# Relaying the hybrid-head stage of a two-block transformer kernel on half chunks

## The reference, cut to what matters

```python
def hybrid_layer(x, ...):
    h = rms_norm_2(x, g_norm)
    z = h @ w_in                         # 2656 columns
    aq, ak, av, ag, bq, bk, bv, bg, cq, ckv, ckr, cg = split(z)
    qa, ka = axial_rope(rms_norm_2(aq, a_qn)), axial_rope(rms_norm_2(ak, a_kn))
    oa = dense_gqa(qa, ka, av) * silu(ag)            # 6 heads, 2 kv heads, 64 wide
    qb, kb = rope(bq), rope(bk)
    ob = windowed_sink_gqa(qb, kb, bv, sink) * silu(bg)
    qc = rms_norm_2(cq, c_qn) @ c_wuq                # 4 heads, 64 + 32 wide
    kv = rms_norm_2(ckv, c_kvn) @ c_wukv
    oc = mla(qc, kv, rope(ckr)) * silu(cg)
    return x + concatenate([oa, ob, oc]) @ w_out     # 1024 by 1024
```

## Time and profile before

| what | value |
|---|---|
| median of three runs | 1870.01 us |
| lowest, highest | 1867.84, 1870.3 us |
| the profiled execution: its time, its span | 1870.01 us, 1868.2 us |
| TensorE busy | 1731.6 us, 93% of the span |
| VectorE busy | 1125.2 us, 60% |
| ScalarE busy | 794.7 us, 43% |
| mean granted TensorE clock | 0.961 of full speed |

### The profile page before, as it was taken

How to read it: one execution, slowest core, us unless ns; L and a number is a source line. 1 busy time by engine, 2 the same in 40 slices (tenths; PEclk the granted TensorE clock), 3 DMA queues, 4 the chain that set the end, 5 groups by cost and what they waited for, 6 DMA issues and landing times.

```text
span 1868.2 us, 28467 instructions
## 1 busy us (share of the span) xinstructions
PE 1731.6 (93%) x12340; PEld 1614.7 (86%) x12340; DVE 1125.2 (60%) x1317; ACT 794.7 (43%) x1011; POOL 41.1 (2%) x64
## 2 busy tenths in 40 slices
PE   7999988888999999999998888899999998889886
PEld 6999888878999999899988778899999997669765
DVE  5444666766766544744466676676545476647663
ACT  5334544333444443543363443344534444434532
POOL 0000000000000000000000000000000010001000
PEclk9999999989999999999999998999999999889978
DMA  7555543433455555555454332354655452215310
GB/s 280 182 184 188 193 181 122 150 113 136 159 180 203 183 192 189 190 192 188 181 199 162 136 139 110 137 179 158 220 186 181 180 210 96 88 59 203 113 45 23
DMA packets 43357, 299.43 MB, mean 160 GB/s; under 512 B 4816, under 2 KB 5216, under 8 KB 8416
## 3 DMA queue, kind: packets, MB, share of 16 engines
q1 hardware_dynamic: 39744, 285.23, 42.2%
q10 hardware_dynamic: 3488, 12.38, 1.9%
...
## 4 chain that ended last, share of the span: by engine, by line
PE 74%; DVE 10%; ACT 8%; issue 5%; DVEq 3%; POOL 1%; DMA 1%; POOLq 0%; ACTq 0%; SPq 0%
PE ps L1373 21%; PE ps L1374 21%; PE ps L1375 21%; DVE wlo L838 3%; ACT whi L536 3%; PE ps L1744 2%; PE ps L1771 2%; DVEq L1119 1%; ACT prob L726 1%; ACT prob L808 1%; PE ps L1459 1%; PE ps L1755 1%; POOL rs L497 1%; PE ps L1460 1%; PE ps L1417 1%
## 5 line engine op out<-in xcount | busy, mean ns | idle before, releaser
L838 DVE TENSOR_TENSOR wlo<-raw,whi 128x2048 fp32r<-128x2048 f32 x270 | 616.8, 2291 | 474.8 <-ACT whi L536 468.2
L1373 PE MATMUL ps<-xhi,whi 128*128 128x256 f32 (+1 forms) x2512 | 724.6, 288 | 0.0
L1374 PE MATMUL ps<-xlo,whi 128*128 128x256 f32 (+1 forms) x2512 | 716.9, 285 | 0.0
L1375 PE MATMUL ps<-xhi,wlo 128*128 128x256 f32 (+1 forms) x2512 | 716.5, 285 | 0.0
L536 ACT ACTIVATE whi<-raw 128x2048 fp32r<-128x2048 f32 x270 | 508.2, 1905 | 17.5 <-DMA raw<-stream 17.0
L1373 PEld LDWEIGHTS ps<-xhi,whi 128*128 128x128 f32 (+1 forms) x2512 | 487.1, 194 | 6.2 <-issue 2.9
L1374 PEld LDWEIGHTS ps<-xlo,whi 128*128 128x128 f32 (+1 forms) x2512 | 486.7, 194 | 3.1 <-issue 0.6
L1375 PEld LDWEIGHTS ps<-xhi,wlo 128*128 128x128 f32 (+1 forms) x2512 | 486.0, 193 | 0.4
L1373 PE MATMUL ps<-whi,yar 128*128 128x512 f32 (+1 forms) x492 | 195.9, 398 | 0.7 <-DVE wlo L838 0.7
L1374 PE MATMUL ps<-wlo,yar 128*128 128x512 f32 (+1 forms) x492 | 192.1, 391 | 0.0
L1375 PE MATMUL ps<-whi,yar 128*128 128x512 f32 (+1 forms) x492 | 191.6, 389 | 0.0
...
## 6 DMA issues: line engine op xcount, KB each, us to landing
raw<-stream SPq DMA_DIRECT2D x270, 1024.0 KB, 4.8
...
```

The lines of the kernel that those rows point to most:

```text
L838: TT(wlo[:, s, :], raw[:, s, :], whi[:, s, :].bitcast(F32), ALU.subtract).then_inc(lo_v, 1)
L1373: pe.matmul(dst, lh, rh, start=first, stop=False)
L1374: pe.matmul(dst, lh, rl, start=False, stop=False)
L1375: return pe.matmul(dst, ll, rh, start=False, stop=last)
```

## The change

It rewrites the order and the work split of the two hybrid layers.

- **Half chunks.** A slot is divided in two; TensorE does 24 of the 48 matmuls of a chunk in each half, and steps can lie on either. Chunks are used in the order 0, 1, 2, 5, 6, 7, 3, 4, 8 to 13. `SLOTS2` places the `scores` and the `turn` with `values` of each group.
- **Values next to turn.** `values` of a group now follows its own `turn` directly, with the `scores` of the next group between them. VectorE's `weigh` moves to the half slot of its `scores`, behind the `split` there, and VectorE's splits come two slots ahead of their use instead of three.
- **Narrow splits.** Loads and both splits take only the columns used (`chunk_width`): 1536 (five times), 1280, 768 and 512 instead of 2048, while ten of the 18 chunks keep 2048.
- **Rotations.** The head norm weights are multiplied into copies of the cosine and sine tables (`ropeg`) once a layer; the head's scale is applied last; each rotation has fewer, wider operations.
- **ScalarE for VectorE.** Squares for the head norms and the latent norms, three of the copies of `z` and the eight copies of `values` (groups 0 to 7) go to ScalarE. The window mask is added in PSUM on the far half alone.
- **Output by token halves.** The product with `w_out` runs for the first token half in four steps `out` inside the list, around the `turn` and `values` of group 9, into banks 0 and 1; the second half comes after, into banks 4 and 5. At the layer boundary the second split moves behind the first half's norm.

```diff
+HCOLS = (0, 1, 2, 5, 6, 7, 3, 4, 8, 9, 10, 11, 12, 13)
...
+        order[a:a + AT_WOUT] = [a + i for i in HCOLS]
...
-HYB_V = (2, 4, 7) + GATES
-HYB_A = tuple(i for i in range(AT_WOUT) if i not in HYB_V)
+HYB_V = GATES
+HYB_A = tuple(i for i in HCOLS if i not in HYB_V)
...
+def chunk_width(c):
+    i = LOAD[c] - BLOCK1_CH
+    if i < 0:
+        return CW
+    i %= LAYER2_CH
+    if i < Z_CH:
+        return KD * Z_CHUNKS[i]
+    return {AT_UQ: 2 * UQ_W, AT_UKV: UKV_W}.get(i, CW)
 GROUPS2 = 10
+SLOTS2 = ((5.5, 6.5), (6.5, 7.5), (7.5, 8), (8, 9), (9, 10), (10, 10.5), (10.5, 11.5), (11.5, 13), (13, 14), (14, 15))
...
-    at(3, "a_rotate")
-    for j in range(2):
-        at(5 + j, "flip", j)
-        at(9, "flip", 2 + j)
-        at(13, "flip", 4 + j)
-        at(14, "flip", 6 + j)
-    at(5, "l_norm")
-    at(7, "l_turn")
-    at(8, "b_rotate")
+        before.setdefault(int(2 * slot), []).append(step)
+    at(3, "a_norm")
+    at(4.5, "flip", 0)
+    at(5, "flip", 1)
+    at(6, "b_rotate")
+    at(8.5, "flip", 2)
+    at(8.5, "flip", 3)
+    at(8, "l_norm")
+    at(9.5, "l_turn")
     at(11, "cq_rotate")
     at(12, "ck_rotate")
-    for g in range(GROUPS2):
-        at(6 + min(g, 8), "scores", g)
-        at(6 + min(g, 8), "exp", g)
-        at(6 + g, "weigh", g)
-        at(7 + g, "turn", g)
-        at(8 + g, "values", g)
+    at(12, "flip", 4)
+    at(12, "flip", 5)
+    at(12.5, "flip", 6)
+    at(12.5, "flip", 7)
+    for g, (a, b) in enumerate(SLOTS2):
+        at(a, "scores", g)
+        at(a, "exp", g)
+        at(a, "weigh", g)
+        at(b, "turn", g)
+        at(b, "values", g)
     at(12, "o_gate", 0)
-    at(15, "o_gate", 1)
-    at(17, "o_gate", 2)
-    rank = {"flip": 0, "l_turn": 0, "turn": 1, "scores": 2, "exp": 2, "values": 3, "weigh": 4}
+    at(14, "o_gate", 1)
+    at(15.5, "o_gate", 2)
+    for p in range(1, 15):
+        at(p + 0.5, "split", p + 2)
+    rank = {"flip": 0, "l_turn": 0, "turn": 1, "scores": 2, "exp": 2, "values": 3, "split": 7, "weigh": 8}
     steps = []
-    for slot in range(18):
-        steps += sorted(before.pop(slot, []), key=lambda x: rank.get(x[0], 6))
-        if slot < AT_WOUT:
-            steps.append(("chunk", slot))
+    for half in range(2 * AT_WOUT + 4):
+        steps += sorted(before.pop(half, []), key=lambda x: rank.get(x[0], 6))
+        if half < 2 * AT_WOUT:
+            steps.append(("chunk", half // 2, HCOLS[half // 2], half % 2))
+        else:
+            steps.append(("out", half - 2 * AT_WOUT))
...
+        def acc_bank(X, t):
+            return 4 * t if X >= 3 * DEPTH else 4 + 2 * t
+        def turn_bank(X, t):
+            return 6 - 4 * t if X > 3 * DEPTH else 4 + 2 * t
...
-                sp.dma_start(raw[:, c % SLOTS, :], stream[LOAD[c]]).then_inc(landed[c % SLOTS], 16)
+                w = chunk_width(c)
+                sp.dma_start(raw[:, c % SLOTS, 0:w], stream[LOAD[c]][:, 0:w]).then_inc(landed[c % SLOTS], 16)
...
+                A(whi[:, s, 0:w], raw[:, s, 0:w], ACT.Copy).then_inc(hi_ready, 1)
...
+                    elif kind == "a_norm":
+                        hyb_taken(act, l, 2)
+                        for t, b in enumerate((tmp, thb)):
+                            A(b[:, 512:1024], z[:, t, Z_AQ:Z_AV], ACT.Square, scale=0.125).then_inc(a_sq, 1)
+                    elif kind == "l_norm":
+                        hyb_taken(act, l, 4)
+                        for t in range(NT):
+                            A(tmp[:, 512:704], z[:, t, Z_CQ:Z_CKV], ACT.Square, scale=192.0 ** -0.5,
+                              accum_out=rq[:, t, 8:9])
+                            A(tmp[:, 704:832], z[:, t, Z_CKV:Z_CKR], ACT.Square, scale=128.0 ** -0.5,
+                              accum_out=rq[:, t, 9:10]).then_inc(rq_ready, 1)
+                            act.drain()
+                    elif kind == "values":
+                        g = step[1]
+                        br, t, kv, ne = group(g)
+                        if br < 2:
+                            act.wait_ge(o_done, l * GROUPS2 + (8 * DEPTH + g + 1))
+                            rows_ = slice(64 * kv, 64 * kv + 64)
+                            A(oAB[rows_, 3 * br:3 * br + 3, t * P:(t + 1) * P],
+                              bank(3)[rows_, 0:3 * P].rearrange("p (m t) -> p m t", m=3), ACT.Copy).then_inc(o_read, 1)
...
+                def turn_pair(x, a, b, heads, tab, sub, n):
+                    cosn, sinn = tab
+                    w = sub * 2 * n
+                    def cut(v):
+                        return v.rearrange("p h (s c n) -> p h s c n", s=sub, c=2)
+                    sin4 = sinn.rearrange("p (s c n) -> p s c n", s=sub, c=2)
+                    TT(a, x, cosn.unsqueeze(1).to_broadcast([P, heads, w]), ALU.mult)
+                    for c in range(2):
+                        if sub == 1:
+                            TT(cut(b)[:, :, 0, c, :], cut(x)[:, :, 0, 1 - c, :],
+                               sin4[:, 0, c, :].unsqueeze(1).to_broadcast([P, heads, n]), ALU.mult)
+                        else:
+                            TT(cut(b)[:, :, :, c, :], cut(x)[:, :, :, 1 - c, :],
+                               sin4[:, :, c, :].unsqueeze(1).to_broadcast([P, heads, sub, n]), ALU.mult)
...
+                    elif kind == "a_norm":
+                        for t, b in enumerate((tmp, thb)):
+                            dve.wait_ge(a_sq, l * 2 + (t + 1))
+                            dve.tensor_reduce(rq[:, t, 0:8], b[:, 512:1024].rearrange("p (e d) -> p e d", e=8), AX, ALU.add)
+                            TS(rtmp[:, t, 0:8], rq[:, t, 0:8], EPS, None, ALU.add).then_inc(rq_ready, 1)
+                            hyb_taken(dve, l, 2)
+                            x = z[:, t, Z_AQ:Z_AV].rearrange("p (e d) -> p e d", e=8)
+                            for e0, e1, o in ((0, 6, 0), (6, 8, 128)):
+                                a, b = (v[:, 64 * e0:64 * e1].rearrange("p (e d) -> p e d", d=64) for v in (thb, tmp))
+                                turn_pair(x[:, e0:e1, :], a, b, e1 - e0,
+                                          (ropeg[:, t, o:o + 64], ropeg[:, t, o + 64:o + 128]), 2, 16)
+                            dve.drain()
+                            TT(thb[:, 0:512], thb[:, 0:512], tmp[:, 0:512], ALU.add)
+                            dve.drain()
+                            TT(x, thb[:, 0:512].rearrange("p (e d) -> p e d", e=8),
+                               rs[:, t, 0:8].unsqueeze(2).to_broadcast([P, 8, 64]), ALU.mult).then_inc(qk_tok, 1)
...
-                            dve.wait_ge(pt_done, l * GROUPS2 + (G - 1))
-                            TT(prob[:, 0:ne, :], sc, win[:, t, :].unsqueeze(1).to_broadcast([P, ne, T]), ALU.add)
+                            far = slice((1 - t) * P, (2 - t) * P)
+                            TT(sc[:, :, far], sc[:, :, far], win[:, t, far].unsqueeze(1).to_broadcast([P, ne, P]), ALU.add)
                             dve.drain()
-                            dve.tensor_reduce(sm[:, 8:8 + ne], prob[:, 0:ne, :], AX, ALU.max)
+                            dve.tensor_reduce(sm[:, 8:8 + ne], sc, AX, ALU.max)
...
+            def rows_of(X, ch, lh, ll, t, final, first, last=False):
+                s = ch % SLOTS
+                wh, wl = wts(whi, s, 2), wts(wlo, s, 2)
+                for a in range(2):
+                    if final and t and a and not last:
+                        turns(X + 1, 0)
+                    for b in range(2):
+                        n, k = (a, b) if final else (b, a)
+                        ins = mm3(bank(acc_bank(X, t) + n), lh[:, k, t * P:(t + 1) * P], ll[:, k, t * P:(t + 1) * P],
+                                  wh[:, k, n * 512:(n + 1) * 512], wl[:, k, n * 512:(n + 1) * 512], first and k == 0,
+                                  final and b == 1)
+                    if final and not (t and a):
+                        ins.then_inc(acc_done, 1)
+                if t:
+                    ins.then_inc(used, 1)
...
+                    if kind == "out":
+                        j = step[1]
+                        ready(wo[j])
+                        pe.wait_ge(y_ready, l * 3 + (4 * DEPTH + (1, 2, 2, 3)[j]))
+                        if j == 0:
+                            hyb_taken(pe, l, HCOLS[-1])
+                            hyb_taken(pe, l, HCOLS[-2])
+                        rows_of(X, wo[j], mhi[:, 2 * j:2 * j + 2, :], mlo[:, 2 * j:2 * j + 2, :], 0, j == 3, j == 0)
...
+                for j in range(4):
+                    rows_of(X, wo[j], mhi[:, 2 * j:2 * j + 2, :], mlo[:, 2 * j:2 * j + 2, :], 1, j == 3, j == 0,
+                            l == DEPTH - 1)
```

286 lines of the change are left out of this document (121 added, 165 removed).

## The result

| | before | after |
|---|---|---|
| median of 4 runs each, us | 1869.40 (1867.84 to 1870.30) | 1835.83 (1832.20 to 1837.64) |
| ratio, 95% interval | 1 | 0.9819 (0.9802 to 0.9836) |
| profiled execution's span, us | 1868.2 | 1834.3 |
| mean granted clock | 0.961 | 0.972 |
| loads, MB | 299.43 | 293.14 |

The account below looks back on a forecast made before the run. It took idle TensorE and its low clock in the two hybrid layers as the bound. Per layer, 24 us off the stretch less 7 of clock loss gives 17; 1870 - 34 = 1836 us, range 1816 to 1858.

Parts of the forecast that it names:

- The ceiling: Both hybrid layers: 128 us of work each at full clock, 38 us excess, so at most 76 us gained, 1794 us.
- The walk: Hybrid layer from third chunk: TensorE's new order against both queues, 14 us idle, stretch 142 instead of 166 us.
- 1, sixth chunk: TensorE arrives at 17.6 us, but the full split behind the rotation is done at 19.2: 1.6 us wait.
- 4, UKV: UKV waits 3.5 us for the copy of UQ's result, which ScalarE makes only after exp 6.
- 5, flip of branch C: Second flip waits 2.2 us for the copy of values 6, now behind exp 7 on ScalarE.
- 6, values 7, 8: In the layer's tail, values 7 and 8 wait for probT behind a split: 0.5 and 0.4 us.
- The rule on ScalarE: If ScalarE's copies of values took three times VectorE's 552 ns: 13 us a layer, time near 1850 us.
- The clock: Low clock costs 7 us a layer instead of 14: one fall at UKV, 5, a smaller in the tail, 2.
- None of this is worth anything by itself: VectorE's and ScalarE's relief counts only where it shortens a chain TensorE waits for; VectorE falls by 18 us a layer.
- The clock stays up: Rival: UKV's wait is shorter or broken up, so no clock fall; 1822 us, 13% with the ceiling included.
- falls as before: Rival: waits in tail and start cost the old 14 us of clock a layer; 1850 us, 22%.
- Slower by ScalarE's queue: Rival: splits ahead of probT copies make ScalarE late everywhere, 15 us a layer; 1880 us, 5%.

Follow-up runs that it names:

- experiment 12: Changed kernel with UQ's and UKV's copies before exp, VectorE's last split earlier, ScalarE's splits before tanh, third gate chunk before UKV: 1816.55 us.
- experiment 7: Changed kernel with ScalarE copying UQ's and UKV's results out of PSUM ahead of the next exp: 1828.41 us.
- experiment 8: Changed kernel with VectorE's split of the last output chunk ahead of the last values and third gate: 1826.50 us.
- experiment 10: Changed kernel with UQ's and UKV's copies before exp, VectorE's last output split before the last values, and ScalarE's gate-chunk splits before tanh: 1818.04 us.
- experiment 3: Changed kernel with the eight copies of values of branches A and B back on VectorE: 1833.83 us.
- experiment 1: Changed kernel with all splits and loads of the hybrid stage 2048 columns wide again: 1839.02 us.
- experiment 5: Changed kernel with full splits, the eight copies of values and all squares back on VectorE; new order kept: 1836.05 us.
- experiment 6: Changed kernel with the step order, last group's buffers and output product of the kernel before, every relief kept: 1858.41 us.

## Why the prediction came out right

**The ceiling.** I put the layer's work at full clock at 128 us. The second layer of experiment 12 has 128.3 us busy at clock 0.99. (One term was rounded up: 20.30 us for 91 matmuls make 21.4 us for 96, not 22.) That step holds, and with it the split of the excess into idle time and clock.

**The walk.** Each wait, forecast against measured in layer 1 / layer 2 of the profile after:

| step of the walk | forecast | measured |
|---|---|---|
| 1, sixth chunk | 1.6 | 1.73 / 1.73 |
| 2, turn 2 | 0.4 | 0.48 / 0.48 |
| 3, values 4 | 1.05 | 1.04 / 1.04 |
| 4, UKV | 3.5 | 3.79 / 3.79 |
| 5, flip of branch C | 2.2 | 2.75 / 2.37 |
| 5, next chunk | 0.6 | 0 / 0.46 |
| 6, values 7, 8 | 0.5, 0.4 | 0.80, 0.80 |
| 6, `out` 1 | 0.9 | 1.27 |
| 6, values 9 | 1.1 | 1.11 |
| 6, `out` 3 | 1.7 | 1.82 |

Sum 14 forecast, 15.7 us idle measured. The two waits for probT at values 7 and 8 are the coarsest. Five of the causes are shown by an edit that takes the wait away: experiment 7 that at UKV, experiment 8 the last, experiment 10 those of values 4, 7 and 8; experiment 3 shrinks that of the flip. For the others the cause is the releaser that the profile names, and no run tests it.

**The durations.** The interpolated splits, 1.76 and 1.48 us, measured 1.755 and 1.482; the mask in PSUM, taken at 0.55 between 0.55 and 0.96, measured 0.567; ScalarE's copy of values, 0.49, measured 0.483. VectorE lost 18.8 us of its 108.2 in the first layer, 18 forecast.

**The rule on ScalarE.** The 384-wide copy takes 0.483 us on ScalarE and took 0.552 on VectorE, and moving the eight copies back changed nothing that can be told (experiment 3). The Trainium skill (ScalarE: Activation LUTs, "Rules for kernel authors") puts simple elementwise work on VectorE, where it is up to about three times faster in bf16. This case's copy, out of PSUM in fp32, does not bear that out, and the 1850 us that I had put on a copy three times slower did not come.

**The clock: right in sum, wrong in place, and the sum in part by luck.** I had 7 us a layer, 5 at UKV and 2 in the tail; measured are 5.6 and 6.7 us over 128 and rather less at UKV. By the rows of layer 1: the sixth chunk's first half took 4.27 us instead of 3.12 (1.2 lost, after a wait of 1.73), UKV 2.90 instead of 1.86 (1.0), the half chunk behind the flip 4.13 instead of 3.11 (1.0), and the 54 matmuls behind the wait for the last split 14.14 us instead of the 12.54 of experiment 3 (1.6). The step that failed is the one that took a stretch with 1.63 us idle at clock 1.00 as a sign that only the wait at UKV would pull the clock down. Waits of 1.73 and 1.82 us did as well, each at 1.2 to 1.6 us.

A longer list of rows would have warned me, for in the trace before the length of a wait does not decide either. The clock fell behind a wait of 1.38 us at 1554.20 and stood at 1.00 behind one of 2.25 us at 1625.45. The line of the first, and the windows of the 4 us behind both:

```profile
1554.20 0.88 PE L1755 MATMUL ps<-cst,prob 128*128 128x128 f32 x6 [1.38 <-DVE prob L1331]
```

```profile
1554.20:1558.20 4.00, 4.00 (x18) 3.07 (x19) 3.09 (x4) 2.36 (x5) 0.00 (x0) 0.73 0.52 213
1625.45:1629.45 4.00, 4.00 (x26) 3.47 (x27) 3.75 (x7) 1.25 (x3) 0.00 (x0) 1.00 0.00 0
```

So a price for the clock at one place is an average over executions. The sum held because the tail was priced at 2 all the same and UKV too high, and because this execution lost the clock at the sixth chunk in both layers, which most of the others did not (see the table in the last section). The same error is in my expectation of experiment 8, 3 to 4 us for what gave 9.3: it priced the wait and left out the clock behind it.

**The end of the kernel.** I had it unchanged. It is 1.0 us shorter, and that belongs to the 33.6 us.

**What the gain comes from.** "None of this is worth anything by itself" was right, within the intervals, of the parts of the relief that experiments 1, 3 and 5 undid in the new order, and too low for the old one: 10.5 us there (experiment 6). In the profiles of that pair TensorE is idle 3.4 us less in the two layers and busy some 9 us less, at a clock of 0.92 and 0.93 in place of 0.89 and 0.90, so most of it came by the clock; how is not shown. In my sum the walk used the lighter VectorE; that the result does not need two thirds of this relief I had not seen.

**The rivals.** "The clock stays up" (1822 us, nothing lost to it) and "falls as before" (1850 us, 14 us a layer) lie on both sides of what was measured, 5.6 and 6.7 us at a clock of 0.95 and 0.94. "Slower by ScalarE's queue" had the right mechanism at a quarter of its price: values wait for probT four times a layer, 3.8 us where the rival had 15, none over 1.11 us. Loads cost nothing, as priced: no wait of TensorE in the stage is put down to one.
